# A hybrid decoder trunk: the layer embedding's input is loaded and turned at the end of the mixer, and its old place holds an expert slot

## What is computed

```python
x = layer_norm(ALPHA * x + mix, ln_g[i, 0], ln_b[i, 0])
ffn = moe(x, router_w, router_b, moe_w_gate[i], moe_w_up[i], moe_w_down[i])
x = layer_norm(ALPHA * x + ffn, ln_g[i, 1], ln_b[i, 1])
emb = p[i] @ ple_w_proj[i]            # p[i]: 256 x 256
gate = sigmoid(x @ ple_w_gate[i] + ple_b_gate[i])
x = x + gate * emb
```

## Time and profile before

| what | value |
|---|---|
| median of 3 runs | 1599.93 us (1598.16 to 1600.61) |
| the profiled execution's own time | 1598.78 us |
| its span | 1596.9 us |
| busy in the span | PE 1575.7 us, PEld 938.0, DVE 743.1, ACT 515.0, POOL 45.6 |
| DMA queue of SP | 530.93 MB, 82.4% of the 16 engines' span |
| DMA queue of POOL | 2.21 MB, 0.4% |
| read from HBM | 532.06 MB, 334 GB/s over the span |
| mean granted clock of PE | 0.999 |

### The profile page before, as it was taken

The page is one execution under the profiler, slowest core; times in us unless marked ns, Lnnn a source line. Parts: engine busy times, 40 slices in busy tenths (PEclk is TensorE's granted clock), DMA queues, the critical chain, the costliest instruction groups (busy, mean ns, idle before and its releaser), DMA issues.

```text
span 1596.9 us, 17946 instructions
## 1 busy us (share of the span) xinstructions
PE 1575.7 (99%) x7472; PEld 938.0 (59%) x7472; DVE 743.1 (47%) x1155; ACT 515.0 (32%) x653; POOL 45.6 (3%) x47
## 2 busy tenths in 40 slices
PE   9999999999999999999999999999999999999998
PEld 7874433378877744333788887643434887434335
DVE  5671222294757622222956755512224667222227
ACT  5521222154433212211544443222212553132113
POOL 0000000000000000001020000000010000000010
PEclk9999999999999999999999999999999999999999
DMA  9879999976536799999755556799999677999992
GB/s 362 339 310 422 421 421 420 421 278 257 182 135 239 309 383 420 422 421 420 311 227 203 183 211 263 313 421 421 421 420 419 239 275 312 375 422 420 422 420 105
DMA packets 75147, 534.41 MB, mean 335 GB/s; under 512 B 8976, under 2 KB 9264, under 8 KB 10544
## 3 DMA queue, kind: packets, MB, share of 16 engines
q1 hardware_dynamic: 73728, 530.93, 82.4%
q0 software_dynamic: 1328, 2.21, 0.4%
HBM read 532.06 MB, written 1.05 MB: 334 GB/s over the span
## 4 chain that ended last, share of the span: by engine, by line
PE 88%; DMA 7%; DVE 4%; ACT 1%; issue 1%; SPq 0%; DVEq 0%; ACTq 0%
PE psum L1092 38%; PE psum L699 11%; PE psum L701 11%; PE psum L700 11%; PE psum L1084 4%; PE psum L710 3%; DMA expert_high<-in_experts 3%; DMA expert_work<-in_experts 3%; PE psum L1044 2%; PE psum L850 2%; DVE w_lo L1621 2%; PE psum L1102 1%; PE psum L1037 1%; DMA raw<-in_slots 1%; PE psum L989 1%; PE psum L934 1%
## 5 line engine op out<-in xcount | busy, mean ns | idle before, releaser
L1621 DVE TENSOR_TENSOR w_lo<-raw,w_hi 128x2048 fp32r<-128x2048 f32 (+1 forms) x128 | 268.2, 2111 | 190.7 <-ACT w_hi L1310 190.3
L1310 ACT ACTIVATE w_hi<-raw 128x2048 fp32r<-128x2048 f32 (+1 forms) x128 | 221.8, 1751 | 156.8 <-PE psum L701 104.8
L699 PE MATMUL psum<-w_hi,xT_hi 128*128 128x512 f32 x672 | 264.9, 394 | 1.0 <-DVE w_lo L1621 1.0
L701 PE MATMUL psum<-w_hi,xT_lo 128*128 128x512 f32 x672 | 261.8, 390 | 0.0
L700 PE MATMUL psum<-w_lo,xT_hi 128*128 128x512 f32 x672 | 261.5, 389 | 0.0
L1310 ACT ACTIVATE work<-psum 128x512 f32<-128x512 f32 x152 | 85.8, 597 | 311.2 <-PE psum L710 208.7
L1092 PE MATMUL psum<-raw,xg 128*64 128x512 f32 x736 | 170.4, 594 | 0.9 <-ACT work L1310 0.5
L1621 DVE TENSOR_TENSOR work_r<-psum,work_r 128x512 fp32r<-128x512 f32 (+1 forms) x100 | 67.6, 688 | 183.0 <-ACT spare_r L1310 98.8
L699 PEld LDWEIGHTS psum<-w_hi,xT_hi 128*128 128x128 f32 x672 | 126.2, 188 | 27.5 <-issue 1.0
L701 PEld LDWEIGHTS psum<-w_hi,xT_lo 128*128 128x128 f32 x672 | 126.1, 188 | 26.7
L700 PEld LDWEIGHTS psum<-w_lo,xT_hi 128*128 128x128 f32 x672 | 126.3, 188 | 25.8 <-issue 0.2
(11 more groups left out here) (175 smaller groups left out, 1714.0 us busy)
## 6 DMA issues: line engine op xcount, KB each, us to landing
raw<-in_experts SPq DMA_DIRECT2D x128, 1024.0 KB, 14.0
raw<-in_slots SPq DMA_DIRECT2D x120, 1024.0 KB, 5.0
expert_work<-in_experts SPq DMA_DIRECT2D x96, 1024.0 KB, 13.2
expert_high<-in_experts SPq DMA_DIRECT2D x68, 1024.0 KB, 12.9
expert_spare<-in_experts SPq DMA_DIRECT2D x24, 1024.0 KB, 13.0
expert_norm<-in_experts SPq DMA_DIRECT2D x20, 1024.0 KB, 10.0
expert_bias<-in_experts SPq DMA_DIRECT2D x20, 1024.0 KB, 9.2
x<-in_experts SPq DMA_DIRECT2D x20, 1024.0 KB, 14.7
```

What stands on the lines that cost most here:

```text
L699: mm(out, lhs[0], rhs[0], start=start, stop=False)
L701: return mm(out, lhs[1], rhs[0], start=False, stop=stop)
L1310: return nc.scalar.activation(dst, src, func)
L1621: return tt(lo, whole, hi.bitcast(F), ALU.subtract)
```

## The change

p is no longer loaded at the start of a layer. `load_p` issues it on POOL near the end of the mixer: in the convolution behind `load_norm` and behind the second turn of the b gate (`mt_in_psum` 8), in the retention behind `load_norm` and when slot 27 is used, in the gating MLP ahead of `load_norm`, when slot 31 is used. It lands in the scratch that later holds `hid`; `pT` lies where `hT` will be. For that the retention's `MISC_IN` moves from working slot 7 to 0 and its split x from 0 to 7. PE turns p between row tiles 0 and 1 of the last three output slots, into bank 7; ACT copies it ahead of x's turned tile; PE waits for it before the first `embed`. The first group of projections loses the turn, the copy and the wait.

The place `emb` is then free until the computed embedding arrives. It keeps expert slot 19, but is loaded ahead: as the eighth early load in the convolution, the eleventh in the retention, the thirteenth in the gating MLP. `BEHIND` issues 14 early loads instead of 13; the other slots keep their places and their order.

```diff
-X_IN = ((0, 1), (0, 1), (5, 8))
+X_IN = ((0, 1), (7, 1), (5, 8))
-MISC_IN = (2, 7, 7)
+MISC_IN = (2, 0, 7)
-BEHIND = [{5: 3, 7: 1, 8: 1, 9: 1, 10: 1, 11: 1, 12: 1, 13: 1, 15: 3},
-          {1: 3, 5: 1, 8: 1, 9: 1, 10: 1, 27: 3, 30: 2, 31: 1},
-          {1: 3, 5: 1, 8: 1, 9: 1, 10: 1, 27: 2, 31: 3, 35: 1},
-          {1: 3, 5: 4, 8: 1, 9: 1, 10: 1, 15: 3}]
+BEHIND = [{5: 3, 6: 1, 7: 1, 8: 1, 9: 1, 10: 1, 11: 1, 12: 1, 13: 1, 15: 3},
+          {1: 3, 5: 1, 8: 1, 9: 1, 10: 1, 27: 4, 30: 2, 31: 1},
+          {1: 3, 5: 1, 8: 1, 9: 1, 10: 1, 27: 2, 31: 3, 35: 2},
+          {1: 3, 5: 5, 8: 1, 9: 1, 10: 1, 15: 3}]
...
-        first = [[*free, *work[:3], *dense, xg, work[3], y],
-                 [*free, *dense, *work[:2], xg, *work[2:], y],
-                 [*free, *dense, work[0], xg, *work[1:], y]][layer % 3]
-        order = [*first, raw[3], tail[0], raw[0], tail[1], raw[1], tail[2], raw[2], ("x", 0), ("emb", 0)]
+        first = [[*free, *work[:3], emb, *dense, xg, work[3], y],
+                 [*free, *dense, *work[:2], xg, emb, *work[2:], y],
+                 [*free, *dense, work[0], xg, *work[1:], emb, y]][layer % 3]
+        order = [*first, raw[3], tail[0], raw[0], tail[1], raw[1], tail[2], raw[2], ("x", 0)]
...
+                p_in=view(M0, T * PLE, "p (t n) -> p t n", t=T),
+                pT=view(M0 + 512, T * PLE, "p (j n) -> p j n", j=2),
...
+                elif kind == "emb" and L % 3 == 0:
+                    if L:
+                        sp.wait_ge(x_tile_ready, 6 * L)
                 elif kind == "emb":
-                    sp.wait_ge(weights_used, n + 1)
+                    sp.wait_ge(*((sT_ready, HEADS) if L % 3 == 1 else (vs_in_psum, 16)))
...
-            pool.wait_ge(slot_full[RAW_OF[1]], 16)
-            pool.dma_start(p_in, A["p"][0, 0].rearrange("(t p) d -> p t d", p=P)).then_inc(p_loaded, 16)
...
+            def load_p(L):
+                pool.dma_start(scratch[L % 3].p_in, A["p"][L, 0].rearrange("(t p) d -> p t d", p=P)).then_inc(p_loaded, 16)
...
                 if L:
                     pool.wait_ge(x_tile_ready, 6 * L)
-                    pool.dma_start(p_in, A["p"][L, 0].rearrange("(t p) d -> p t d", p=P)).then_inc(p_loaded, 16)
...
                     pool.wait_ge(weights_used, starts[L][0] + 32)
+                    load_p(L)
                 load_norm(L, 0)
+                if L % 3 == 0:
+                    pool.wait_ge(mt_in_psum[L], 8)
+                    load_p(L)
+                elif L % 3 == 1:
+                    pool.wait_ge(weights_used, starts[L][0] + 28)
+                    load_p(L)
...
-                        last = nc.tensor.transpose(psum[:, 3, j * SEQ + t * P:j * SEQ + (t + 1) * P],
+                        last = nc.tensor.transpose(psum[:, 7, j * SEQ + t * P:j * SEQ + (t + 1) * P],
...
                 for i in range(4):
-                    if i == 2:
-                        pe.wait_ge(pt_ready, L + 1)
                     project_slot(L, 0, 1, i)
-                    if i == 0:
-                        turn_p(L)
...
                 for t in range(T):
+                    if t:
+                        turn_p(L)
                     for i in range(1, 4):
...
+                pe.wait_ge(pt_ready, L + 1)
                 for i in range(3):
                     embed(0, i)
...
-                    if (q, b, t) == (0, 0, 1):
-                        act.wait_ge(pt_in_psum, L + 1)
-                        copy(pT, psum[:, 3, :].rearrange("p (j n) -> p j n", j=2)).then_inc(pt_ready, 1)
...
                 split_behind(starts[L][1] - 3)
+                act.wait_ge(pt_in_psum, L + 1)
+                copy(scratch[L % 3].pT, psum[:, 7, :].rearrange("p (j n) -> p j n", j=2)).then_inc(pt_ready, 1)
                 save_tile(3 * L + 1, 0)
```

More of the change, by code:

```diff
@@ L118, in expert_places @@
         tail = [("high", HIGH_OF[n - 3 + i]) for i in range(3)]
-        work, xg, y = [("work", i) for i in range(4)], ("xg", 1), ("y", 0)
+        work, xg, y, emb = [("work", i) for i in range(4)], ("xg", 1), ("y", 0), ("emb", 0)
         free = [("spare", 0), ("spare", 1), ("norm", 0), ("bias", 0)]
         dense = [raw[4], raw[5], high[0]]
-        first = [[*free, *work[:3], *dense, xg, work[3], y],
-                 [*free, *dense, *work[:2], xg, *work[2:], y],
-                 [*free, *dense, work[0], xg, *work[1:], y]][layer % 3]
-        order = [*first, raw[3], tail[0], raw[0], tail[1], raw[1], tail[2], raw[2], ("x", 0), ("emb", 0)]
+        first = [[*free, *work[:3], emb, *dense, xg, work[3], y],
+                 [*free, *dense, *work[:2], xg, emb, *work[2:], y],
+                 [*free, *dense, work[0], xg, *work[1:], emb, y]][layer % 3]
+        order = [*first, raw[3], tail[0], raw[0], tail[1], raw[1], tail[2], raw[2], ("x", 0)]
         n_first = len(order)
-        once = {("spare", 0): SPARE_K, xg: EARLY_K, y: LATE_K, ("emb", 0): LAST_K}
+        once = {("spare", 0): SPARE_K, xg: EARLY_K, y: LATE_K, emb: LAST_K}
         turns = iter([k for k in range(n_first) if k not in once.values()])
@@ L316, in tiles @@
             return v.rearrange("p (j n) -> p j n", n=P)
-        Scratch = namedtuple("Scratch", "x_split pick kept norm y hid hT place pw cmp1 cmp2 sums w_over")
+        Scratch = namedtuple("Scratch", "p_in pT x_split pick kept norm y hid hT place pw cmp1 cmp2 sums w_over")
         def scratch_of(kind):
@@ L374, in build @@
         decay = emb[:, 0, :].rearrange("p (h n) -> p h n", h=HEADS)
-        p_in = emb[:, 1, 0:T * PLE].rearrange("p (t n) -> p t n", t=T)
-        pT = emb[:, 1, 512:1024].rearrange("p (j n) -> p j n", j=2)
         s_ident, s_const = sem("identity_loaded"), sem("constants_loaded")
@@ L742, in turn_p @@
             def turn_p(L):
+                p_in = scratch[L % 3].p_in
                 pe.wait_ge(p_loaded, 16 * (L + 1))
@@ L1043, in embed @@
                     c, j = divmod(i, 2)
-                    last = mm(psum[:, 2 * t + c, :], pT[:, j, t * P:(t + 1) * P], whole[:, 2 * j + c, :],
+                    last = mm(psum[:, 2 * t + c, :], scratch[L % 3].pT[:, j, t * P:(t + 1) * P], whole[:, 2 * j + c, :],
                               start=j == 0, stop=j == 1)
```

## The result

The changed kernel takes 1602.2 us (median of 20 runs, 1599.65 to 1606.12), the kernel before, measured beside it, 1599.6 (20 runs): ratio 1.0018, 95% interval 1.0011 to 1.0024. It is 2.6 us slower. The forecast was 1590.8 in a range of 1588.4 to 1595.5: wrong in sign and outside its range.

The account below looks back on a forecast made before the run. It took DMA to bound the expert stages (2.5 us a slot against PE's 1.72). Terms -8.1 - 0.8 - 0.8 + 0.6 = -9.1 us, against the median 1599.93, gave 1590.8 us, range 1588.4 to 1595.5.

Parts of the forecast that it names:

- The backlog is at least 2.3 us, so between 2.3 and 2.5 us of advance survive: Expert stages: shortest landing 7.2 us less 4.9 for an empty queue, so later loads keep nearly all their 2.5 us advance.
- the gain of 8.1: Ends of the four expert stages: PE's waits for late expert slots, 3 x 1.98 + 2.17 us, all vanish.
- Rival 3: Expert stages: an empty queue costs 6 us, so 1.2 us of advance survive, 4.8 in all; 1594 us, chance 8%.
- Cost 0 in the mixers of layers 0 and 3: Slot 7 lands up to 2.5 us later in layer 0, but its split stays hidden; layer 3 alike; cost 0.
- Rival 2: Mixers lose at a dense slot what the stage wins, 2.5 us a layer; about 1600 us, chance 8%.
- the bound of 1 us: Layer 1's mixer, extra MB ahead of slots 28 and 29: cost 0, at most 2.5 less 1.5 swallowed by a wait.
- Layer 1's p, 0.6 us between 0 and 1.2,: Layer 1's mixer end: p's 0.26 MB, served beside slot 31's load, costs 0.6 us of DMA time.
- Layer 3's wait, 0.8: Layer 3: PE's wait for p at its old place is removed, gain 0.8 us.
- layer 2's port, 0.8: Layer 2: norm spread delayed, so slot 35's split runs in 2.3 us instead of 3.94; gain 0.8, between 0 and 0.8.
- DVE first: Layer 2: DVE's split starts before POOL's spread and holds the shared port to its end; no row showed this case.
- Rival 1: Mixers' ends: p lands late and PE waits at its turn; up to 22 us lost, 1613 us, chance 4%.

Follow-up runs that it names:

- p later: Layer 1's p issued when slot 28 is used instead of 27: on the p only kernel 1597.15 us (0.9986), on the changed kernel 1602.30, again 1601.29.
- p only: The changed kernel with the emb slot loaded late again, as before the change, p keeping its new place: 1599.57 us, 0.9994 of before.
- the change's second profile: Profile of the changed kernel run once more, unaltered, beside two others on one chip: 1603.11 us, 1.0023 of before.

## Why the prediction was wrong

- **"The backlog is at least 2.3 us, so between 2.3 and 2.5 us of advance survive"** failed, and with it the gain of 8.1. I took 4.9 us for a load that meets an empty queue from a load that stood alone. The load issued at 134.7, with one load and the last 0.2 us of another outstanding, took 6.9 us (7.3 before): 0.4 us survived, and behind it in layer 0 nothing; in layer 3 the loads from 22 us on came 1.4 us late. The step took the backlog of one load for the lead that all would keep, and took the rate for constant as long as the queue isn't empty. It never was, and yet the rate fell to 354 to 398 GB/s for 24 us, which costs more than was won: 2 to 4.5 us more over the four stages by the profiles (774.3 to 774.8 where the load is late, 776.5 to 779.0 where it is early) and 4.4 by medians. The early load brings no storage: the places are the same 22, PE frees them when it did, and a queue that was fed by the late load goes short instead.
- **Rival 3, the queue runs dry,** came nearest to the mechanism, at 8%, but the queue ran thin and not dry. Its size was too small (1.2 us of advance left, 1594), and it had no row for a loss beyond the advance. The range's high end, made from it, adds up to 1595.8 and not 1595.5; the result lies beyond either.
- **Cost 0 in the mixers of layers 0 and 3** was argued for slot 7, where it holds. The load issued at 66 us has no such room: it came 0.9 to 2.5 us later in three of six profiles, and PE waited up to 2.28 us behind it. Rival 2 had the mechanism; its mean stays open. Layer 3's mixer shows none of it (144.5 to 144.9 us from stage 2 to stage 3 in all six). In layer 1 the bound of 1 us held: with p later the stretch is 251.6 and 252.0 with the MB early, 251.2 with it late.
- **Layer 1's p, 0.6 us between 0 and 1.2,** was mis-sized. Slot 31 landed later by 1.3 us with the change (9.1 against 7.8), 1.6 with p only, 2.0 in the change's second profile (9.8), but only 0.4 with the emb slot behind the dense loads (8.2), for 0.6 us of transfer; and behind PE waits of 1.7 to 2.9 us came the slow clock, which was in no term. Price by runs: 1.8 and 2.4 us.
- **Layer 3's wait, 0.8, and layer 2's port, 0.8,** held: -0.69 and -0.87 in the profiles. With the emb load late and p out of slot 31's way the p part gives 2.6 us. DVE first was the case that no row had shown; the Trainium skill, SBUF — State Buffer, section Who interferes with whom, says the first to start holds the port to its end, and this trace agrees: split 2.29, spread 3.16 us.
- **Rival 1, p late,** did not come: no execution profiled shows a PE wait for p.

## What to carry to other kernels

Before a load is moved ahead, ask whether it adds storage or only empties the queue at the hour when it was the filler: look at the loads issued right behind the consumer's longest gap, not at the shortest time of the whole stage. Here that load took 7.3 us before and 6.9 after, so it had 0.4 us to give and not 2.5. Keep a small transfer of another queue away from the one load that the matmul engine is about to wait for, and put nothing ahead of that load that isn't wanted sooner. A wait of 2 us costs more than 2 us when the clock falls behind it, as it did here in some executions.

## What the runs showed of the hardware

- Fewer bytes can be slower: with 4.2 MB more, loaded early for nothing and again late, the kernel was 3.3 us faster than with the early load alone, because the late load kept the queue full when the stage began. Against the kernel with the late load alone the useless MB seem to cost (0.9997 and 0.9986 of before, on two chips).
- With 2.5 loads of 1 MB outstanding on average instead of 3.4, and over the 8 us behind that, the engines moved 354 to 398 GB/s in layer 0 against 418 to 429, at a busy share of still 0.91 to 0.98.
- 0.26 MB from POOL's queue beside a 1 MB load of SP's: that load took 8.2 to 9.8 us in the six profiles that have it (9.1 in the mean), 7.1 to 8.5 in the six that don't and have two expert loads just ahead of it all the same (7.7). The difference of 1.4 us is over twice p's own transfer of 0.6. The Trainium skill, DMA: Bandwidth & Descriptors, section Queues, rings and completion order, has the engines take turns between queues packet by packet; the trace agrees that p gets in beside the load, and shows that the price is not its share of bytes.
- At PE waits of 2.87, 2.38, 2.28 and 1.98 us the granted clock fell to 0.50, during the wait or within about 1 us of its end; after waits of 1.96 and 1.69 it fell some 20 us later, in `route`. After waits of 0.3 to 1.3 us it did not, and no profile without one of these six waits shows such a fall before the last 10 us of the kernel. Each fall lasted 3.4 us, the one at 2.87 us 6.8.
